# A causal mask made by a predicated copy on VectorE instead of a matmul, with a new order of steps in two attentions (one Trainium2 core)

## The reference, cut to what matters

```
def block(args):                       # one block of 128 queries, all heads
    s = einsum('bhqd,bhkd->bhqk', qi, k) * scale
    s = s + cqi[..., None] - c[:, :, None, :]          # c: running sum of log forget gates
    s = where(kpos[None, :] <= qpos[:, None], s, -inf) # later keys are masked
    pr = softmax(s, axis=-1)
    return einsum('bhqk,bhkd->bhqd', pr, v)
```

## Time and profile before

| what | value |
|---|---|
| median of three runs | 2512.32 us |
| the profiled execution, its own time | 2510.95 us |
| its span | 2509.1 us |
| TensorE matmul busy | 2473.6 us (99%), 11658 matmuls |
| TensorE weight loads busy | 2017.6 us (80%) |
| VectorE busy | 1539.0 us (61%) |
| ScalarE busy | 1097.2 us (44%) |
| GpSimd busy | 1320.2 us (53%) |
| granted TensorE clock | 1.0 of full speed in all slices |
| first attention | about 656 to 931 us of the span |
| second attention | about 1145 to 1655 us of the span |

### The profile page before, as it was taken

How to read it: one execution, slowest core, us unless ns; L and a number is a source line. 1 busy time by engine, 2 the same in 40 slices (tenths; PEclk the granted TensorE clock), 3 DMA queues, 4 the chain that set the end, 5 groups by cost and what they waited for, 6 DMA issues and landing times. The chain is left out here.

```text
span 2509.1 us, 36104 instructions
## 1 busy us (share of the span) xinstructions
PE 2473.6 (99%) x11658; PEld 2017.6 (80%) x11658; DVE 1539.0 (61%) x2240; ACT 1097.2 (44%) x2016; POOL 1320.2 (53%) x1092
## 2 busy tenths in 40 slices
PE   8999999999999999999999999999999999999999
PEld 5788888888788878888888888777778888878777
DVE  6555552344677785435666666646668777776785
ACT  4332333301766661116777777832432333344441
POOL 3788887433455554432111111144289888666683
PEclk9999999999999999999999999999999999999999
DMA  3222223579210015321111111331133333387552
GB/s 111 88 75 64 70 67 110 179 259 324 83 34 25 25 34 184 126 100 60 43 42 42 42 42 43 122 122 51 52 108 116 114 118 113 139 271 215 180 185 79
DMA packets 126499, 267.24 MB, mean 107 GB/s; under 512 B 13873, under 2 KB 14001, under 8 KB 126401
## 3 DMA queue, kind: packets, MB, share of 16 engines
q1 hardware_dynamic: 84800, 157.85, 20.0%
q10 hardware_dynamic: 41600, 108.19, 12.1%
HBM read 198.02 MB, written 67.96 MB: 106 GB/s over the span
## 5 line engine op out<-in xcount | busy, mean ns | idle before, releaser
L641 POOL TENSOR_SCALAR whi<-raw 128x512 fp32r<-128x512 f32 x194 | 138.4, 713 | 803.4 <-PE bank L869 397.5
L643 POOL TENSOR_TENSOR wlo<-raw,whi 128x512 fp32r<-128x512 f32 x194 | 274.3, 1414 | 16.2
L806 PE MATMUL bank<-a_hi,whi 128*128 128x512 f32 x464 | 184.7, 398 | 1.8 <-issue 1.5
L806 PE MATMUL bank<-b_lo,whi 128*128 128x512 f32 x464 | 183.3, 395 | 0.0
L656 POOL TENSOR_TENSOR wlo<-a,whi 128x512 fp32r<-128x512 f32 x114 | 166.5, 1460 | 18.4 <-ACT whi L1693 17.7
L869 PE MATMUL bank<-b_hi,whi 128*128 128x512 f32 x384 | 156.9, 409 | 0.0
L869 PE MATMUL bank<-b_hi,wlo 128*128 128x512 f32 x384 | 151.5, 395 | 0.0
L869 PE MATMUL bank<-b_lo,whi 128*128 128x512 f32 x384 | 151.2, 394 | 0.0
L806 PE MATMUL bank<-b_hi,whi 128*128 128x512 f32 x336 | 133.3, 397 | 0.4 <-DVE b_lo L2306 0.4
L806 PE MATMUL bank<-a_hi,wlo 128*128 128x512 f32 x336 | 132.6, 395 | 0.0
L806 PE MATMUL bank<-a_lo,whi 128*128 128x512 f32 x336 | 132.6, 394 | 0.0
(11 more groups left out here) (710 smaller groups left out, 7633.1 us busy)
## 6 DMA issues: line engine op xcount, KB each, us to landing
raw<-in_w SPq DMA_DIRECT2D x206, 256.0 KB, 2.6
a<-in_pairs SPq DMA_DIRECT2D x152, 256.0 KB, 2.7
wd_scr<-wd SPq DMA_DIRECT2D x55, 256.0 KB, 5.1
wd<-in_down SPq DMA_DIRECT2D x44, 256.0 KB, 4.6
xs_scr<-made ACTq DMA_DIRECT2D x40, 256.0 KB, 2.6
fc<-c_scr ACTq DMA_DIRECT2D x16, 512.0 KB, 3.5
h_scr<-up_y ACTq DMA_DIRECT2D x13, 512.0 KB, 2.6
raw<-wd_scr SPq DMA_DIRECT2D x26, 256.0 KB, 2.8
```

The lines of the kernel that those rows point to most:

```text
L641: nc.gpsimd.tensor_scalar(hi, src, 1.0, 1.0, ALU.mult, ALU.mult).then_inc(w_hi, 1)
L643: nc.gpsimd.tensor_tensor(lo, src, hi.bitcast(F32), ALU.subtract).then_inc(w_lo, 1)
L806: last = nc.tensor.matmul(psum_ap, ws[w][:, k, :], a[:, kt, hs(h)], start=(first and i == 0 and j == 0), stop=(final and i == n - 1 and j ...
```

## The change

1. **Second attention, mask.** The mask matmul (L1035) goes. VectorE instead copies -1e30 (`never`, a part of `mask_r`) over the last 128 columns of the scores where `later_keys` is not zero: `mask(s)`, a predicated copy of 128x128 into PSUM, 16 in a pair. It stands one step ahead of the maxima that need it: in step s `mask(s+3)` just before the reciprocal `inverse(s+2)`; where `scores(s+3)` comes after the fillers, at the next step's start before `maxima`.
2. **Maxima.** The reduction now takes the minimum of c - score, so it leaves `neg_max` itself; L2509 and its semaphore go, `expo` has scale=-1, and c is stored with the other sign. The explicit wait for the transposes before `maxima` goes too.
3. **High parts ahead.** On ScalarE in steps with s % 8 of 5 or 6 (but not 14) the first chunk's `high` stands before `normalise(s+1)`.
4. **Written out.** The loops over pairs on ScalarE and VectorE become Python loops: the instructions stand one after the other.
5. **First attention.** ScalarE takes `high(2)` before `expo(3)`, VectorE `low(2)` before `normalise(3)`, TensorE `flip_p(2)` before `mean_square(1)`, and the fillers around are divided otherwise. In the last pair `merge_part` goes tile by tile over both halves, and VectorE's `window_lo(1)` comes after `add(2)`.

```diff
@@ TensorE, second attention
-                    pe.wait_ge(fx.max, st + max(s - 1, 0))
+                    pe.wait_ge(fx.neg_max, st + max(s - 1, 0))
...
-                        if c + n == w:
-                            nc.tensor.matmul(score[s % 2][:, w - P:w], ident_r[:], mask_r[:, P:2 * P], start=False, stop=False)
@@ ScalarE, second attention
-                    nc.scalar.activation(fp[s % 3][:, 0:w], fp[s % 3][:, 0:w], ACT.Exp, bias=neg_max[:, one],
+                    nc.scalar.activation(fp[s % 3][:, 0:w], fp[s % 3][:, 0:w], ACT.Exp, bias=neg_max[:, one], scale=-1.0,
...
+                    ahead = s % 8 in (5, 6) and s != NST - 2
+                    if ahead:
+                        high(CHUNKS_OF[s][0])
                     if s + 1 < NST and s != NST - 2 and (fills or s > 0):
                         normalise(s + 1)
...
-                    for n in CHUNKS_OF[s]:
+                    for n in CHUNKS_OF[s][ahead:]:
                         high(n)
...
-            for pp in range(2):
-                forget_pair(0, pp, True)
-            with act.Fori(1, NPAIR // 2 - 1) as it:
+            for it in range(NPAIR // 2 - 1):
@@ VectorE, second attention
+                def mask(s):
+                    w = (STEPS[s][1] + 1) * P
+                    dve.wait_ge(fx.scored, st + (s + 1))
+                    settle()
+                    v.copy_predicated(score[s % 2][:, w - P:w], later_keys, never).then_inc(fx.masked, 1)
...
-                    dve.wait_ge(fx.flipped, ch + (CHUNKS_OF[s - 3][-1] + 1 if s >= 3 else 0))
-                    dve.wait_ge(fx.scored, st + (s + 1))
+                    dve.wait_ge(fx.masked, st + (s + 1))
                     settle()
-
                     v.tensor_tensor_reduce(out=fp[s % 3][:, 0:w], in0=score[s % 2][:, 0:w], in1=fc[hh][:, 0:w],
-                                           scale=SCALE, scalar=-3.0e38, op0=ALU.subtract, op1=ALU.max,
-                                           accum_out=mx[:, one]).then_inc(fx.max, 1)
-                    dve.wait_ge(fx.max, st + (s + 1))
-                    v.tensor_scalar(neg_max[:, one], mx[:, one], -1.0, None, ALU.mult).then_inc(fx.neg_max, 1)
+                                           scale=-SCALE, scalar=3.0e38, op0=ALU.add, op1=ALU.min,
+                                           accum_out=neg_max[:, one]).then_inc(fx.neg_max, 1)
...
                     if fills and s in LEAVES and s < NST - 2:
                         forget_out(*following, LEAVES[s])
+                        mask(s + 2)
...
+                    if s + 3 < NST and not (fills and s + 1 in LEAVES):
+                        mask(s + 3)
                     if s + 2 < NST:
                         inverse(s + 2)
...
-            with dve.Fori(0, NPAIR // 2 - 1) as it:
+            for it in range(NPAIR // 2 - 1):
@@ ScalarE, first attention
+                high(2)
                 expo(3)
                 log_mean(score[0][:, 0:HALF], n, 1, s_sq)
-                high(2)
@@ VectorE, first attention
+                low(2)
                 normalise(3)
-                low(2)
@@ TensorE, first attention
-                fill(1, 0, range(2))
+                fill(1, 0, range(1))
+                pe.wait_ge(sw.q_std, n * 2 + 1)
+                flip_p(2)
+                fill(1, 0, range(1, 2))
                 pe.wait_ge(sw.exp, st * 4 + 12)
                 mean_square(n, 1, score[0][:, 0:HALF], s_sq)
-                fill(1, 0, range(2, 3))
-                pe.wait_ge(sw.q_std, n * 2 + 1)
-                flip_p(2)
-                fill(1, 0, range(3, KT))
+                fill(1, 0, range(2, KT))
                 values(2)
```

More of the change, by code:

```diff
@@ L160, in __init__ @@
         self.scored = sem(n + "_scored")
-        self.max = sem(n + "_max")
         self.neg_max = sem(n + "_neg_max")
@@ L179, in __init__ @@
         super().__init__(sem, n)
+        self.max = sem(n + "_max")
         self.q_sq = sem(n + "_q_sq")
@@ L189, in __init__ @@
         self.g_out = sem(n + "_g_out")
+class ForgetSemaphores(AttentionSemaphores):
+    def __init__(self, sem, n):
+        super().__init__(sem, n)
+        self.masked = sem(n + "_masked")
 STEPS = [(hh, qb) for hh in range(2) for qb in range(NB)]
@@ L408, in build @@
         n0, n1, n2 = NormSemaphores(sem, "n0"), LayerNormSemaphores(sem, "n1"), LayerNormSemaphores(sem, "n2")
-        sw, fx = WindowSemaphores(sem, "sw"), AttentionSemaphores(sem, "fx")
+        sw, fx = WindowSemaphores(sem, "sw"), ForgetSemaphores(sem, "fx")
         chain_step = sem("chain_step")
@@ L963, in window_pair @@
                     values(2)
-                    for c, h in ((0, 0), (0, 1), (1, 0)):
-                        merge_part(c, h, range(2))
+                    for k in range(2):
+                        for h in range(2):
+                            merge_part(0, h, range(k, k + 1))
+                    merge_part(1, 0, range(2))
                     values(3)
@@ L971, in window_pair @@
                 scores(2)
-                fill(0, 1, range(2))
+                fill(0, 1, range(3))
                 pe.wait_ge(sw.lo, st + 1)
@@ L976, in window_pair @@
                 flip_p(1)
-                fill(0, 1, range(2, 7))
+                fill(0, 1, range(3, 7))
                 scores(3)
@@ L1628, in forget_pair @@
                     if fills and s in (9, 15):
-                        act.wait_ge(fx.max, st + (8 if s == 9 else 16))
+                        act.wait_ge(fx.neg_max, st + (8 if s == 9 else 16))
                         sums_in(*following, s // 15)
@@ L2338, in window_lo @@
                 v.tensor_tensor(b_hi[:, j, :], s_o[:, j, :], b_lo[:, j, :].bitcast(F32), ALU.subtract).then_inc(sw.o_lo, 1)
+            later_keys = mask_r[:, P:2 * P].bitcast(mybir.dt.int32)
+            never = mask_r[:, 2 * P:3 * P].bitcast(F32)
             own_valid = mask_r[:, 0:P].bitcast(mybir.dt.int32).unsqueeze(1).to_broadcast([P, 4, P])
@@ L2420, in window_pair @@
                     low(2)
-                    window_lo(1)
                     gate(1)
                     add(2)
+                    window_lo(1)
                     low(3)
@@ L2527, in add @@
                                     f_fold[0:DH, :], ALU.add).then_inc(fx.o, 1)
+                mask(0)
                 maxima(0)
+                mask(1)
                 inverse(0)
@@ L2535, in forget_pair @@
                 v_lo(fx, fv, flips[0][:], 0, it * 4 + 2 * pp)
+                mask(2)
                 for s in range(NST):
@@ L2835, in _ @@
             dve.wait_ge(chain_step, 5 * KT + 5)
-            v.tensor_scalar(fp1[0:16, :], fp0[0:16, :], 1.0 / SCALE, None, ALU.mult).then_inc(chain_step, 1)
+            v.tensor_scalar(fp1[0:16, :], fp0[0:16, :], -1.0 / SCALE, None, ALU.mult).then_inc(chain_step, 1)
             forget_out(0, 0, 1, bank[1])
```

## The result

The changed kernel took 2519.05 us (median, 2518.44 to 2521.18) against 2512.2 of the kernel before on the same chip: ratio 1.0031, 95% interval 1.0022 to 1.0039. It is slower by 0.3%, though TensorE has 128 matmuls less. The profiled execution has a span of 2516.7 us, 7.6 more than before.

The account below looks back on a forecast made before the run. TensorE was taken to set the end. 2510.95 + 10.7 (seven full pairs) + 1 (last pair) - 3.5 - 0.3 (first attention) = 2518.9; with 1.37 to the median 2520.2, said as 2520 us, range 2503 to 2526.

Parts of the forecast that it names:

- Mask matmuls, 1.04 us a pair: Second attention, TensorE: removing 128 mask matmuls frees 1.04 us a pair, 8.3 us over eight pairs, if waits end earlier too.
- The add waits: Second attention: values of steps 5 and 13 wait until VectorE's add empties the bank, 3.4 us over 12 places.
- Rival C: Second attention: add waits go altogether (3.4 us) and the whole mask gain stays, 2497 us; chance 0.08.
- The copy hidden in a full pair: VectorE, second attention: 0.29 us a copy, mostly where VectorE idles; with L2509 gone, costed at nothing in a full pair.
- rival E: VectorE: a mask copy costs as the wide one (0.70 us), 2526 us and up to 2530 with the last pair; chance 0.06.
- Written-out loops at nothing: ScalarE and VectorE loops over pairs written out: costed at nothing, could give or take 0.1 us a pair, 1 us in all.
- Step 6 at +1.17: Full pair, ScalarE: high waits for step 5's values with normalise(7) behind it, so step 7's values start 1.17 us later.
- The 0.5 us of the second half go into the next wait.: Full pair, second attention: the masks' 0.5 us gain of the second half is spent in the next wait.
- Last pair at +1: Second attention's last pair, without fillers: shorter chain (0.19 us a step) against the same exchanges, +1 us, between -1 and +3.
- First attention at -3.8: First attention: step 2's wait for GpSimd's last select goes, -0.5 us in seven pairs (-3.5); last pair -0.3.
- B (2504): Rival: exchange free because normalise(7) may be 1.7 us late without a stall; half the mask gain kept, 2504 us; chance 0.20.
- The signs: Expected in the profile: values 5 to 7 about 7.2 us apart, normalise(7) delayed, select's wait gone, pair 62.9 against, 64.9 for.

Follow-up runs that it names:

- run 1: Changed kernel with the exchange taken out (every high part back behind its normalise): 2508.16 us, ratio 0.9987 to the kernel before.
- run 2: Changed kernel with the exchange only in steps 5 and 13, not in step 6: 2514.01 us, ratio 1.0010 to the kernel before.
- run 3: Changed kernel with the exchange only in step 6: 2514.37 us, ratio 1.0011 to the kernel before.
- run 9: run 5 with ScalarE's fold and VectorE's add one step earlier, in steps 4, 8 and 12 of full pairs: 2510.74 us, ratio 0.9996.
- run 5: run 1 with the last pair's mask again a matmul, no predicated copy there: 2506.27 us, ratio 0.9977 to the kernel before.
- run 8: Changed kernel with the loops over pairs on ScalarE and VectorE kept as before: 2523.75 us, ratio 1.0045 to the kernel before.
- run 10: run 5 with the last pair of the first attention as in the kernel before: 2505.73 us, ratio 0.9976 to the kernel before.
- run 11: run 9 with the exchange in steps 5 and 13 of full pairs added: 2503.82 us, ratio 0.9967 to the kernel before.
- run 4: Kernel before with parts 1 and 2 alone (predicated copy, minimum), loops and first attention as before: 2513.04 us, ratio 1.0006.

## Why the prediction came out right, step by step

The forecast was 2520 and slower; it is 2519.05 and slower. Its mechanism, an exchange that costs more than the masks give back, is shown by runs 1 to 3. That its sum is met to 1 us is luck. Measured less forecast, by the distances in the traces: full pairs -4.06, the way to the last pair +0.38, the last pair +1.62, the start of the second attention +2.14, the rest -0.4; together -0.3.

- **Mask matmuls, 1.04 us a pair.** Borne out as far as it can be seen: from values 1 to 3, 7 to 9 and 15 to 1 the changed pair is shorter by 0.26, 0.17 and 0.53, and the narrow score's two products start 0.06 us apart where it was 0.17. That half is kept without the exchange was forecast as 0.55 and measured as 0.46 to 0.54 a pair (run 1).
- **The add waits.** The 3.4 us of the earlier trace rows were read as time that matmuls lose. They are idle time of weight loads; no matmul of a full pair had a wait for the add, and the loads of the transposes had 4.8 us in 16 places for low parts beside it, which the forecast didn't weigh. Rival C's price of 3.4 us was not there to be won, and run 9, in which those waits are gone, gained nothing.
- **The copy hidden in a full pair.** Right for its size (median 290 ns, 0.29 said) and by run 1. In the last pair it isn't hidden: one copy there takes 1.08 us in the chain (run 5). Eight of the 128 copies were dearer than rival E's 0.70 (1.08 to 1.14).
- **Written-out loops at nothing.** Wrong: 4.7 us (run 8). The argument compared two stretches of the kernel before, where a jump costs VectorE 0.20 us; it said nothing of a loop with other instructions in it. Against the kernel before the error doesn't show: the kernel before has no such stall, and neither has the changed one.
- **Step 5 at -0.06.** Nearly right: from values 1 to values 5 the pair needs 12.90 us, 12.87 before.
- **Step 6 at +1.17.** Right in mechanism, +0.86 in size. The chain was added with full durations; on VectorE an operation started 0.08 to 0.1 us before the shown end of the one ahead there, and the reciprocal of step 8 came 0.19 us after the copy's start, not 0.29.
- **Step 13 at +0.42.** +0.51.
- **"The 0.5 us of the second half go into the next wait."** Wrong, and the largest error of a full pair: from values 15 to 1 the pair gains 0.53, because TensorE meets no new wait there. So a full pair costs +0.85 on average where I had +1.5, 5.1 us in pairs 0 to 5 where the forecast gives 9.2.
- **Last pair at +1.** The last pair alone lost 2.6, and the way into it took 1.1 more than a full pair of the changed kernel: the copy in an idle chain and TensorE's clock, which run 5 doesn't separate, and the exchange, which costs 2.2 us of the last pair (56.47 for 54.31 in run 1).
- **First attention at -3.8.** The start of the second attention is 1.7 us earlier: six pairs gain 0.20 us each, the seventh 0.86, and the last loses 0.35. The select's wait of 0.34 us went as said, but the bank's wait behind it (0.31) was not seen, and the last pair's part is nothing (run 10). Two selects took 1.09 and 1.61 us here, yet they were done in time; so the rule of the Trainium skill (GPSIMD Engine Reference, Key points) that the forecast named didn't decide the size.
- **Rivals.** B (2504) was the version without the exchange as it turned out: run 1, 2508, short of it by what the last pair and the first attention lost. As the change stands, its condition (`normalise(7)` may be late) failed: the transposes of step 7 wait 0.17 us for that row.
- **The signs.** `high` waits for the values of step 5 with `normalise(7)` behind it, and the select's wait is gone, as said. A full pair of 64.2 us lies between the two marks (62.9 against the argument, 64.9 for it), and the distance from values 5 to 7 is 6.89 where 7.2 was said: the argument on step 6 holds with about three quarters of its size.

## What to carry to other kernels

An exchange of two instructions on an engine pays only if what is put first is ready first; look for the wait that the moved instruction will end, and for what then stands behind it. The same exchange was worth +0.6 and -1.0 us a pair, depending on whether fold and add stood behind it (runs 1, 2, 9 and 11), so an exchange that was rejected once can be worth trying again after a change around it. A removed TensorE instruction is worth its time only between waits: half of 1.04 us a pair was kept, and in a stretch where TensorE is idle anyway the work that took its place cost more.

## What the runs showed of the hardware that was not expected

- TensorE's clock fell to 0.5 after a few us in which it was busy for about half, in a pair where it had been at 1.00; idle times of 0.93, 0.93 and 0.23 us that grew to 1.38, 1.04 and 0.77 went ahead of it (run 1; the expectation of run 5 has larger figures for the same waits). The kernel before was busy for 1.07 us in each of two stretches of 2 us at the same place and kept its clock; what tipped it wasn't tried by itself.
- A loop's jump cost VectorE 2.67 us or 0.20, by what the loop held (runs 4 and 8). Written-out code has a price too, 0.35 us once, from values 9 to 11 of pair 2 (6.40 for 6.05) in all kernels with it but none with loops; its cause was not tried.
- The predicated copy of 128x128 took 281 to 1136 ns. In the changed kernel the 97 that had no GpSimd operation beside them took 281 to 301 ns. The 23 that began while one was under way took 340 to 1136 ns, and all ended about 0.15 us after it; in run 1 above the same is seen. Eight began up to 0.08 us ahead of a GpSimd TENSOR_TENSOR and took 289 to 291 ns, as here (VectorE, then GpSimd, of the changed kernel):

```profile
1346.49 0.29 DVE L2508 COPY_PREDICATED score<-mask_r 128x128 f32<-128x128 int32 x1
```

```profile
1346.57 1.35 POOL L649 TENSOR_TENSOR wlo<-raw,whi 128x512 fp32r<-128x512 f32 x1
```

The copy reads its mask and its value from SBUF. The Trainium skill (GPSIMD Engine Reference, Key points) names instructions with two SBUF inputs as those that contend with GpSimd, and these rows agree. The long ones cost a full pair nothing that its distances show (values 7 to 9 are 0.17 us closer than before); in the last pair one stood in the chain.
